# Summing the modulation's products over the 128 partitions: eight one-column matmuls per weight group, against VectorE's 32x32 transpose, a reduction, and four matmuls once a layer

## What is computed

```
mod(l, v) = silu(c_v) @ w_mod[l] + b_mod[l]      # v = 0 latents, v = 1 context; 6144 numbers each
```

## Time and profile before

| | |
|---|---|
| runs | 3, median 3897.05 us (3896.26 to 3897.45) |
| profiled execution: span from its first to its last instruction | 3896.9 us |
| what lies around the span, by the median of the runs | about 0.15 us |
| PE busy | 3769.5 us, 97% of the span |
| DVE, ACT, POOL busy | 2122.0, 1859.7, 1754.3 us |
| mean granted TensorE clock | 0.981 of full speed |

### The profile page before, as it was taken

How to read it: one execution, slowest core, us unless ns; L and a number is a source line. 1 busy time by engine, 2 the same in 40 slices (tenths; PEclk the granted TensorE clock), 3 DMA queues, 4 the chain that set the end, 5 groups by cost and what they waited for, 6 DMA issues and landing times.

```text
span 3896.9 us, 59459 instructions
## 1 busy us (share of the span) xinstructions
PE 3769.5 (97%) x20276; PEld 3069.3 (79%) x20276; DVE 2122.0 (54%) x3273; ACT 1859.7 (48%) x3560; POOL 1754.3 (45%) x1373
## 2 busy tenths in 40 slices
PE   8999899999999998999999999999999999999999
PEld 7866688788888767887888877778888987778887
DVE  4567632776535676327765764742236856553224
ACT  4555544433445654444334534744445652654443
POOL 4423573555544235645555233065564135025564
PEclk9998999999999989999999999999999999999999
DMA  4210241455222202415553322132223542012222
GB/s 138 92 60 28 76 141 60 159 177 172 92 91 87 68 21 82 141 62 165 178 162 108 126 91 87 45 104 97 97 92 119 173 141 76 12 33 87 97 97 87
DMA packets 107773, 391.54 MB, mean 100 GB/s; under 512 B 11952, under 2 KB 12080, under 8 KB 107184
## 3 DMA queue, kind: packets, MB, share of 16 engines
q1 hardware_dynamic: 88704, 321.95, 25.1%
q10 hardware_dynamic: 16416, 57.62, 4.6%
q0 software_dynamic: 2448, 9.24, 0.7%
HBM read 386.67 MB, written 2.10 MB: 100 GB/s over the span
## 4 chain that ended last, share of the span: by engine, by line
PE 69%; issue 17%; POOL 6%; DVE 5%; ACT 2%; DMA 0%; POOLq 0%; ACTq 0%; DVEq 0%; SPq 0%
PE ps L668 18%; PE ps L670 18%; PE ps L669 18%; POOL arena_parts L632 3%; PE ps L1151 2%; POOL arena_parts L636 1%; PE ps L1170 1%; PE ps L1867 1%; POOL lines L423 1%; PE ps L1159 1%; PE ps L2168 1%; PE ps L2074 1%; PE ps L2178 1%; PE ps L1129 1%; PE ps L895 1%
## 5 line engine op out<-in xcount | busy, mean ns | idle before, releaser
L632 POOL TENSOR_TENSOR arena_parts<-ring,arena_parts 128x512 fp32r<-128x512 f32 x498 | 662.4, 1330 | 1172.4 <-ACT arena_parts L609 965.1
L669 PE MATMUL ps<-arena_parts 128*128 128x512 f32 (+1 forms) x3184 | 1185.9, 372 | 0.0
L668 PE MATMUL ps<-h_parts,arena_parts 128*128 128x512 f32 x2128 | 844.3, 397 | 10.0 <-POOL arena_parts L632 7.2
L670 PE MATMUL ps<-h_parts,arena_parts 128*128 128x512 f32 x2128 | 829.7, 390 | 0.0
L636 POOL TENSOR_TENSOR arena_parts<-ring,arena_parts 128x512 fp32r<-128x512 f32 x498 | 672.1, 1350 | 297.1 <-ACT arena_parts L618 296.5
L1648 DVE SCALAR_TENSOR_TENSOR conv<-ps,cols,conv 128x511 f32<-128x511 f32 (+3 forms) x536 | 377.6, 704 | 617.2 <-ACT conv L1663 452.7
L609 ACT ACTIVATE arena_parts<-ring 128x512 fp32r<-128x512 f32 x580 | 364.9, 629 | 698.8 <-PE ps L670 641.0
L669 PEld LDWEIGHTS ps<-arena_parts 128*128 128x128 f32 x3184 | 602.5, 189 | 105.1 <-issue 2.6
L618 ACT ACTIVATE arena_parts<-ring 128x512 fp32r<-128x512 f32 x580 | 363.8, 628 | 609.0 <-PE ps L670 566.8
L668 PEld LDWEIGHTS ps<-h_parts,arena_parts 128*128 128x128 f32 x2128 | 400.3, 188 | 101.2 <-issue 9.7
L670 PEld LDWEIGHTS ps<-h_parts,arena_parts 128*128 128x128 f32 x2128 | 400.2, 188 | 84.3
(11 more groups left out here) (342 smaller groups left out, 6535.2 us busy)
## 6 DMA issues: line engine op xcount, KB each, us to landing
ring<-in_stream SPq DMA_DIRECT2D x612, 512.0 KB, 3.3
ctx<-in_mod ACTq DMA_DIRECT2D x48, 512.0 KB, 3.6
sq<-in_mod ACTq DMA_DIRECT2D x48, 512.0 KB, 3.6
sq<-in_bias POOLq DMA_DIRECT2D x8, 512.0 KB, 4.4
conv<-in_bias POOLq DMA_DIRECT2D x8, 512.0 KB, 4.6
arena<-in_mem ACTq DMA_DIRECT2D x2, 1024.0 KB, 4.8
out_y<-x ACTq DMA_DIRECT2D x8, 256.0 KB, 2.7
x<-in_x SPq DMA_DIRECT2D x4, 256.0 KB, 4.6
```

Source lines behind the costliest of these rows:

```text
L632: eng.tensor_tensor(side_of(lin, i, c, 0, to), side_of(lin, i, c, 0, raw), side_of(lin, i, c, 0, top), ALU.subtract)\
L668: pe.matmul(out, w_h, x_h, start=start, stop=False)
L669: pe.matmul(out, w_h, x_r, start=False, stop=False)
L670: return pe.matmul(out, w_r, x_h, start=False, stop=stop)
```

## The change

`mod_sum_pe` is no longer called for each group. In its place DVE does two instructions a group, and TensorE four matmuls a layer:

- `mod_turn_dve` transposes both vectors of a group at once: 128 x 1024 in squares of 32 x 32, from the first half of `hc` into its second half. After it, a row of partition r in a square holds what 32 partitions had for one feature.
- `mod_fold_dve` adds each run of 32 numbers: 128 x 1024 to 128 x 32, written to `mod_sums`, which lies in a padding tensor (`lead`) that was unused.
- `mod_sum_pe`, once a layer behind tile 8 of `down`, adds the four groups of 32 partitions that remain, for all 12 groups at once: 96 columns, four matmuls that accumulate, with a window of a 128 x 224 constant as the stationary operand.
- `mod_add_dve`, once a layer, adds the bias for all of it: 128 x 96.

DVE turns group i-1 behind tile 0 of iteration i and folds it behind tile 1. Group 10 is turned and folded behind split 0 of `down`, group 11 behind split 5. The table of constants grows by 224 columns (the POOL-queue DMA of 128 x 1664 becomes 128 x 1888 at the start). Counts of semaphores follow.

```diff
+FOLD_AT = SIN_AT + SEQ
+SQUARE = 32
+N_CONST = FOLD_AT + 2 * P - SQUARE
...
+        mod_both, mod_turned = (spare[1][:, 2 * i:2 * i + 2, :].rearrange("p a b -> p (a b)") for i in range(2))
+        mod_sums = lead[:, 0:MOD_GROUPS * MOD_SUMS].rearrange("p (g n) -> p g n", n=MOD_SUMS)
...
-            pe.wait_ge(S["mod_step"], at * STEPS + STEPS)
-            wait(pe, "mod_ready", at)
-            for q in range(4):
-                for v in range(2):
-                    mm = pe.matmul(ps[:, 7, 2 * q + v:2 * q + v + 1], mod_whole[v][:, q * P:(q + 1) * P], ones[:, 0:1], start=True, stop=True)
...
+        def mod_turn_dve(dve, l, g):
...
+            dve.wait_ge(S["mod_step"], at * STEPS + STEPS)
+            wait(dve, "mod_folded", at)
+            dve.transpose(mod_turned, mod_both).then_inc(S["mod_turned"], 1)
+
+        def mod_fold_dve(dve, l, g):
...
+            dve.wait_ge(S["mod_turned"], at + 1)
+            wait(dve, "mod_ready", l)
...
+            dve.tensor_reduce(to, mod_turned.rearrange("p (b n) -> p b n", n=SQUARE), AX.X, ALU.add).then_inc(S["mod_folded"], 1)
+
+        def mod_sum_pe(pe, l):
+
+            pe.wait_ge(S["mod_folded"], MOD_GROUPS * (l + 1))
+            wait(pe, "mod_ready", l)
+            for q in range(P // SQUARE):
+                at = FOLD_AT + P - SQUARE - q * SQUARE
+                mm = pe.matmul(ps[:, 7, 0:2 * 4 * MOD_GROUPS], const[:, at:at + P], mod_sums.rearrange("p g (n q) -> p (g n) q", q=P // SQUARE)[:, :, q],
+                               start=q == 0, stop=q == P // SQUARE - 1)
...
-            return {1: lambda: mod_sum_pe(pe, l, LAST - 1), 8: lambda: mod_sum_pe(pe, l, LAST)}
+            return {8: lambda: mod_sum_pe(pe, l)}
...
-                if j == 3 and not (isinstance(i, int) and i == 0):
-                    mod_add_dve(dve, l, i - 1)
+                if j in (0, 1) and not (isinstance(i, int) and i == 0):
+                    (mod_fold_dve if j else mod_turn_dve)(dve, l, i - 1)
...
-                then.update({5: lambda: mod_add_dve(dve, l, LAST - 1), 9: last})
+                then.update({0: lambda: folded(LAST - 1), 5: lambda: folded(LAST), 9: last})
```

More of the change, by code:

```diff
@@ L161, in build @@
         LINE = 2048
-        sb("lead", [P, (LINE - (nc.sbuf_base + 31) // 32 * 32 % LINE) // 4])
+        lead = sb("lead", [P, (LINE - (nc.sbuf_base + 31) // 32 * 32 % LINE) // 4])
         ring = sb("ring", [P, RING, TILE])
@@ L1852, in mod_tile_dve @@
                     if last:
-                        wait(dve, "mod_summed", at)
+                        wait(dve, "mod_turned", at)
                     if n < 2:
@@ L1870, in mod_add_dve @@
-        def mod_add_dve(dve, l, g):
-            at = group_at(l, g)
-            dve.wait_ge(S["mod_summed"], at + 1)
-            if isinstance(g, int):
-                to, bias = mod[:, l, 4 * g:4 * g + 4, :], cols[:, COL["b_mod", l] + 4 * g:COL["b_mod", l] + 4 * g + 4]
-            else:
-                to, bias = mod[:, l, bass.ds(g * 4, 4), :], cols[:, bass.ds(g * 4 + COL["b_mod", l], 4)]
-            dve.tensor_tensor(to, ps[:, 7, 0:8].rearrange("p (q v) -> p q v", v=2), bias.unsqueeze(2).to_broadcast([P, 4, 2]), ALU.add)\
-               .then_inc(S["mod_ready"], 1)
+            dve.wait_ge(S["mod_step"], at * STEPS + STEPS)
@@ new lines, in mod_turn_dve @@
+            wait(dve, "mod_folded", at)
+            dve.transpose(mod_turned, mod_both).then_inc(S["mod_turned"], 1)
+        def mod_fold_dve(dve, l, g):
+            at = group_at(l, g)
+            dve.wait_ge(S["mod_turned"], at + 1)
+            wait(dve, "mod_ready", l)
+            to = mod_sums[:, g, :] if isinstance(g, int) else mod_sums[:, bass.ds(g, 1), :].rearrange("p g n -> p (g n)")
+            dve.tensor_reduce(to, mod_turned.rearrange("p (b n) -> p b n", n=SQUARE), AX.X, ALU.add).then_inc(S["mod_folded"], 1)
@@ L1881, in mod_gain_dve, with mod_add_dve @@
+        def mod_add_dve(dve, l):
+            dve.wait_ge(S["mod_summed"], l + 1)
+            bias = cols[:, COL["b_mod", l]:COL["b_mod", l] + 6 * KD].rearrange("p (g q) -> p g q", q=4)
+            dve.tensor_tensor(mod[:, l, :, :].rearrange("p (g q) v -> p g q v", q=4), ps[:, 7, 0:2 * 4 * MOD_GROUPS].rearrange("p (g v q) -> p g q v", v=2, q=4),
+                              bias.unsqueeze(3).to_broadcast([P, MOD_GROUPS, 4, 2]), ALU.add).then_inc(S["mod_ready"], 1)
         def mod_gain_dve(dve, l):
-            dve.wait_ge(S["mod_ready"], MOD_GROUPS * (l + 1))
+            dve.wait_ge(S["mod_ready"], l + 1)
@@ L1890, in build @@
         LAST = MOD_GROUPS - 1
-        def mod_up_pe(pe, l):
-            def hook(i, j):
-                if isinstance(i, int) and i == 0:
-                    return
-                if j == 1:
-                    mod_sum_pe(pe, l, i - 1)
-            return hook
         def mod_down_pe(pe, l):
-            return {1: lambda: mod_sum_pe(pe, l, LAST - 1), 8: lambda: mod_sum_pe(pe, l, LAST)}
+            return {8: lambda: mod_sum_pe(pe, l)}
         def mod_up_dve(dve, l):
@@ L2593, in _ @@
                 linear_pe(pe, L["mo", l], pair_of(of(o_high), HP), SEQ, lambda k: [("mo_evac", l * MEM_HEADS + max(k // 2, MEM_HEADS - 2) + 1)])
-                linear_pe(pe, L["up", l], pair_of(HP, rest_of(rest_ffn)), SEQ, hook=mod_up_pe(pe, l), after=banks_of(L["mo", l]),
+                linear_pe(pe, L["up", l], pair_of(HP, rest_of(rest_ffn)), SEQ, after=banks_of(L["mo", l]),
                           twin=n["ffn"], pre=PRE["up", l], between={0: lambda: norm_pe(pe, n["ffn"]), 1: lambda: spread_pe(pe, n["ffn"])})
@@ L2603, in _ @@
                     hook[20] = lambda: norm_pe(pe, final, range(4))
-                down_pe(pe, ("down", l), SEQ, lambda half: [("mod_ready", MOD_GROUPS * (l + 1))] if half else [], hook)
+                down_pe(pe, ("down", l), SEQ, lambda half: [("mod_ready", l + 1)] if half else [], hook)
             halves_done = L["down", LAYERS - 1].chunk0 + 4
@@ L3120, in pack_constants @@
     out[:, SIN_AT:SIN_AT + SEQ] = np.sin(ang).T[np.arange(P) % half]
+    out[:, FOLD_AT + P - SQUARE:FOLD_AT + P] = i % SQUARE == np.arange(SQUARE)[None, :]
     return out
```

12 lines of the change are left out of this document (7 added, 5 removed).

## The result

The changed kernel takes 3851.72 us (median of 4 runs, 3848.67 to 3854.12). The kernel before takes 3897.25 us beside it (3896.26 to 3898.61). The ratio is 0.9881, 95% interval 0.9868 to 0.9893: 45.5 us less. The sign and nine tenths of the size are as forecast. The sum of 41.2 us lacks some 4 us: 2.5 to 5, by the three measurements.

What follows compares the result with a forecast made beforehand. PE, busy 97% of the span and throughout the loop, was taken as the bound. Terms of -44.4, +2.0 and +1.2 gave -41.2 us from the 3896.9 us span, plus 0.15 to the median: 3855.8 us, range 3852 to 3863.

Steps and rivals of the forecast that it cites:

- The sum: Whole kernel: -44.4 from PE, +2.0 new matmuls, +1.2 stall give -41.2 us, so 3855.8 us.
- Removed from PE, 1.85 us each: Loops and `down`: 24 summings leave PE at 1.85 us each, -44.4 us.
- Eight records of 96 columns, +1.0 a layer: New PE matmuls in `down`: 0.85 us plus 0.15 slower start, +2.0 us in all, bounds 0 to 3.7.
- Transpose and reduction: New DVE pair: 1.22 us each, 2.45 us a group, hidden in the loop's 4.6 us of room, cost 0.
- Start of `up`, 0: DVE comes late at the start of `up`, yet no added PE wait: 0, upper bound 1.5 us a layer.
- Stall at tile 2, 0.6 a layer: Tile 2 of `down`: PE waits for DVE's split that a summing used to cover, +1.2 us for two layers.
- Behind `down` all is as before, only earlier: Stages after `down`: claimed unchanged apart from starting earlier, with no term in the sum.
- The 0.15 us between span and median: Whole kernel: median of the runs taken as 0.15 us above the span, turning 3855.7 into 3855.8 us.
- contention: Rival, loop: DVE's new work slows POOL's weight splits and itself, PE waits, +10 us, 3866; chance 0.04.
- an engine that takes over the loop: Rival, loop: transpose at RECIPROCAL's rate, 6.7 us, makes DVE the bound, slower at 3941 us; chance 0.03.
- a dearer pair: Rival, DVE: transpose and reduction at 2.13 us each, folds in `down` overrun, adding 4 us, 3860; chance 0.11.
- that the time is not PE's to give: Rival, summings: they cost only their issue gap or slow later matmuls, gain 10 us, 3887; chance 0.02.

Runs made afterwards that it cites:

- the three measurements: The changed kernel, unedited, measured three times against the kernel before: 3851.72, 3853.76 and 3851.99 us.
- the two further measurements: The changed kernel run twice more without edit: 3853.76 us (ratio 0.9888 to the kernel before) and 3851.99 us (0.9879).
- the third repeat: The changed kernel once more, no edit, measured a third time: 3851.99 us, kernel before 3898.2 us, ratio 0.9879.
- the repeat of before: The kernel before run again with no edit, with a second profile: 3897.12 us, ratio 1.0.
- the threefold transpose: The changed kernel with each DVE transpose made three times, one waiting for the other: 3862.43 us, ratio 0.9906 to the kernel before.

## Why the prediction was right or wrong

1. **Removed from PE, 1.85 us each: right.** ACT's instructions lie 1.85 us closer together per iteration, ten times in each layer; nine iterations take 195.84 us where 195.8 was forecast.
2. **Eight records of 96 columns, +1.0 a layer: too low.** They stand at 987.32 and the next matmul at 988.56, 1.24 us later, at 155 ns a record in place of the 106 taken from 128 columns. Why fewer columns cost more was not tested. That matmul then takes 0.54 us in place of 0.39. By ACT's instructions the whole is 1.42 us, so +2.8 in place of +2.0, within its bounds.
3. **Transpose and reduction: right.** 1.24 + 1.21 us, and hidden in the loop. No row had shown a transpose: 1.22 us was an argued choice between 0.97 and 6.7, and the trace bears it out. The room for them was put too low, at 4.6 in place of 5.1.
4. **Start of `up`, 0: right.** The wait of 3.6 us is the same.
5. **Stall at tile 2, 0.6 a layer: nearly.** PE waits 0.43 us, the whole is 0.71. Moving ACT's load alone took this wait away, which bears out the path that was named for it. No other tile of `down` waits.
6. **The sum.** -44.4 + 2.8 + 1.4 = -40.2; by the stages it is -40.1, against -41.2. By this alone the time would have been 3897 - 40 = 3857, within the range.
7. **"Behind `down` all is as before, only earlier": this is the step that failed.** The sum had nothing for the stages that the change does not touch. Their instructions are the same and come in the same order, but the clock granted to them is not. Of the 45.5 us between the medians, 5.4 lie outside the two stages of `up` and `down` (3.6 and 6.1 in the two further measurements). In the third repeat, whose time is near the median, the fifth stage gives 3.3 us and the seventh 1.0, both behind `down` and both with less half clock. The fifth stage's part came in all three profiles of the changed kernel; of the seventh stage's 4.1 us in the first profile, 3.1 were that execution's. Why the clock falls as it does there stays open. The last 2.1 us, against the repeat of before, lie in the first stage, ahead of the change, and are not the clock's: it has 41.0 us of half clock against 37.5, and PE is idle 36.6 us in it against 39.5. This stage took 709.4 to 712.1 us over all the profiles, so that part is the chance of a run. The range let the clock be "granted a little sooner" only as one of several things on its lower side, down to 3852, and together with items 2 and 5 being nothing; it had no term of its own of -3 to -7 us.
8. **The 0.15 us between span and median** came of one execution. Each execution is some 2.0 us longer than its span (3896.4 and 3898.37 in the repeat of before; 3847.3 and 3849.42 after). The execution that I read was some 2 us slower than the median of its kernel, which hid this. The forecast is not touched, since the sum was made against the median as well; but the 49.6 us between the two spans shown are more than the change's worth for this reason, 1.9 of them in the first stage.

That the result lies only 0.3 us below the range says little by itself: the further medians of 3853.8 and 3852.0 are at its edge or within it. The forecast lacks the same term for all three.

The rivals: contention, an engine that takes over the loop, and a dearer pair are refuted by the loop's rows and by the threefold transpose; that the time is not PE's to give by the kernel with one matmul of eight. The issue gap of 25 ns that the Trainium skill ("TensorE: Matmul & The Clock Gate", Back-to-back issue gap) lists for up to 64 columns does not describe these matmuls, each with a weight load of its own; the Trainium skill says in the same section that this gap leaves out the weight load. The trace agrees: two records alone still lengthen the iteration by 0.24 us.

## What to carry to other kernels

Where TensorE is busy all the time, do not price a small matmul by its columns. Here a record took 106 ns with one column and with 128, each with a weight load of its own; that the weight load sets this time fits, but no run held the weights still to show it. Move such sums to an engine with idle time: 24 x 2.45 us on VectorE gave TensorE back 24 x 1.85 and cost it 4.2 us, for the new matmuls and one short wait a layer. Then look at what stands ahead of a shared queue's next item: two waits that cost nearly 5 us a layer came from loads and steps that stood one chunk too early, and two chunks later was too late again. And give a forecast of a few tenths of a per cent a term for the clock in the stages that are only shifted, some us in either direction, and measure the spread of such stages before you put a difference down to the change.

## What the runs showed of the hardware that was not expected

- The half-clock time in unchanged stages moves when the work ahead of them shifts by 2 us (6.8 us in place of 3.4 behind eight idle matmuls), and it can differ from run to run: 13.7 or 23.9 us in one stage of one and the same kernel, worth 3.1 us. The Trainium skill ("TensorE: Matmul & The Clock Gate", What's actually happening) says that the number of matmuls at the slow clock differs from run to run of the same kernel. The trace agrees: 523 matmuls in 80 us at a clock of 0.94 in one execution, 499 at 0.85 in another.
- A pause of 3.6 us of PE was followed by 3.4 us at half clock, and one of 1.0 us at the same place was not. But a pause of 1.4 us with eight records of 96 columns behind it was, in both layers. In the kernel with 16 one-column matmuls in a row (3.6 us in which PE is recorded as busy throughout) the clock fell for 3.4 us soon after them, while behind eight (1.8 us) it did not.
- VectorE's 32 x 32 transpose of plain f32, 128 x 1024, takes 1.236 us, 2% more than a reduction of as many numbers (1.214).
- A plain f32 record of 96 columns took 155 ns (eight in 1.24 us), one of 128 columns in another place 106 ns. The cause was not tested.
- The matmul behind a row of small ones is recorded with 0.54 us in place of 0.39 behind the 96-column records.
